# Seven loops written out in Python become loops with a counter in an engine's register

## The reference

```
u    = rmsnorm(x) ; proj = u @ w_in                 # q k v, indexer, z, x/B/C, dt
att  = sparse attention over the top-k keys          # prompt, and samples with a paged cache
y    = Mamba-2 scan of x, B, C, dt, gated and normed
h    = x + concat(att, y) @ w_out
f    = rmsnorm(h)
h    = h + (silu(f @ w_gate) * (f @ w_up)) @ w_down  # hidden width 5632
out  = rmsnorm(h)
```

## Time and profile before

| | |
|---|---|
| median of three runs | 3165.68 us |
| the profiled execution | 3167.28 us, the highest of the three |
| its span, first to last instruction | 3164.5 us |
| outside the span | 2.8 us |
| instructions recorded | 51192 |
| PE busy | 2943.7 us, 93% of the span, 20687 matmuls and as many weight loads |
| DVE busy | 1495.3 us, 47% |
| ACT busy | 950.1 us, 30% |
| POOL busy | 547.6 us, 17% |
| DMA | 352.87 MB, mean 112 GB/s |

### The profile page before, as it was taken

How to read it: one execution, slowest core, us unless ns; L and a number is a source line. 1 busy time by engine, 2 the same in 40 slices (tenths; PEclk the granted TensorE clock), 3 DMA queues, 4 the chain that set the end, 5 groups by cost and what they waited for, 6 DMA issues and landing times.

```text
span 3164.5 us, 51192 instructions
## 1 busy us (share of the span) xinstructions
PE 2943.7 (93%) x20687; PEld 2783.8 (88%) x20687; DVE 1495.3 (47%) x2285; ACT 950.1 (30%) x1442; POOL 547.6 (17%) x230
## 2 busy tenths in 40 slices
PE   6999997799999998699689999999999999999997
PEld 5887897677787877499689999999999999999997
DVE  2322598523434333211576767676676752323223
ACT  4223211222222222222334343343434332222222
POOL 1322232111111110034100000000000023334332
PEclk8999999789999888699899999999999999999999
DMA  6422223443454442443222333333232352232321
GB/s 192 112 65 74 82 88 89 119 133 105 114 149 132 132 126 78 155 135 125 76 88 99 119 101 109 118 100 114 96 122 96 116 197 110 96 122 107 113 96 60
DMA packets 366470, 352.87 MB, mean 112 GB/s; under 512 B 40669, under 2 KB 320261, under 8 KB 365016
## 3 DMA queue, kind: packets, MB, share of 16 engines
q1 hardware_dynamic: 333272, 324.61, 32.5%
q10 hardware_dynamic: 33024, 25.77, 2.5%
HBM read 302.59 MB, written 49.13 MB: 111 GB/s over the span
## 4 chain that ended last, share of the span: by engine, by line
PE 55%; issue 35%; POOL 7%; DVE 2%; ACTq 1%; ACT 1%; POOLq 0%; DVEq 0%
PE PS L1222 31%; PE PS L1204 18%; PE PS L797 6%; POOL WL L700 4%; POOL WL L729 3%; ACTq L1266 0%; DVE XR L2250 0%; ACTq L1267 0%; DVE xo_t L2255 0%; DVE xo_x L2255 0%; DVE y_out L2325 0%; POOL WL L721 0%; ACT WRAW L1275 0%; DVE rstd L2243 0%; PE PS L812 0%
## 5 line engine op out<-in xcount | busy, mean ns | idle before, releaser
L797 PE MATMUL PS<-AH,WH 128*128 128x288 f32 (+1 forms) x2208 | 494.0, 306 | 22.4 <-DVE AL L2152 7.2
L1204 PE MATMUL PS<-H,WH 128*128 128x288 f32 x2816 | 489.4, 296 | 0.7 <-DVE us L2217 0.7
L797 PE MATMUL PS<-AL,WH 128*128 128x288 f32 (+1 forms) x2208 | 482.1, 301 | 0.0
L797 PE MATMUL PS<-AH,WL 128*128 128x288 f32 (+1 forms) x2208 | 481.6, 300 | 0.0
L719 POOL TENSOR_TENSOR WL<-WRAW,WH 128x1024 fp32r<-128x1024 f32 x88 | 214.1, 2433 | 1378.6 <-ACT WH L712 1378.6
L1204 PEld LDWEIGHTS PS<-H,WH 128*128 128x128 f32 x2816 | 414.5, 189 | 0.9 <-issue 0.9
L797 PEld LDWEIGHTS PS<-AH,WH 128*128 128x128 f32 (+1 forms) x2208 | 365.8, 194 | 47.9 <-issue 30.0
L1222 PE MATMUL PS<-xo_t,WH 128*128 128x288 f32 x1888 | 380.2, 296 | 8.6 <-ACT kept L1623 7.6
L797 PEld LDWEIGHTS PS<-AL,WH 128*128 128x128 f32 (+1 forms) x2208 | 365.2, 194 | 0.0
L797 PEld LDWEIGHTS PS<-AH,WL 128*128 128x128 f32 (+1 forms) x2208 | 364.5, 193 | 0.0
L2311 DVE TENSOR_TENSOR XD<-PS,XD 128x576 f32<-128x576 f32 x176 | 133.4, 758 | 398.8 <-PE PS L1204 398.8
(11 more groups left out here) (346 smaller groups left out, 4005.3 us busy)
## 6 DMA issues: line engine op xcount, KB each, us to landing
WRAW<-in_w_gate SPq DMA_DIRECT2D x22, 2048.0 KB
WRAW<-in_w_up SPq DMA_DIRECT2D x22, 2048.0 KB
WRAW<-in_w_down SPq DMA_DIRECT2D x22, 2048.0 KB
WRAW<-in_w_in SPq DMA_DIRECT2D x14, 2048.0 KB, 8.6
raw<-in_w_in SPq DMA_DIRECT2D x48, 512.0 KB, 4.1
kca<-in_cache_k SPq DMA_DIRECT2D x256, 64.0 KB, 2.0
vca<-in_cache_v SPq DMA_DIRECT2D x256, 64.0 KB, 2.0
WRAW<-in_w_out SPq DMA_DIRECT2D x16, 1024.0 KB
```

The lines of the kernel that those rows point to most:

```text
L797: last = nc.tensor.matmul(G[gslot][0:width, h, 0:HALF], wt[:, half, k % 8, 0:width], act[:, (k + shift) % KT, h * HALF:(h + 1) * HALF], st ...
L1204: last = mm(G[(slot + t) % 2][:, h, 0:HALF], wt[:, half, 2 * k + t, :], hid[:, m, k, h * HALF:(h + 1) * HALF], start=(k == 0 and wt is WH ...
```

## The change

Seven `for ... in range(...)` become `with engine.Fori(...) as ...`: one on SP, two each on PE, ACT and DVE. The bodies stay as they are, with the loop variable now a register's value. POOL's loops aren't touched. The order of matmuls, casts, subtractions and DMAs on every engine is the same as before, turn for turn.

```diff
@@ SP, load and store of the gate and up stage @@
-            for p in range(1, NPAIR // 2):
+            with sp.Fori(1, NPAIR // 2) as p:
                 for f, w in enumerate(("w_gate", "w_up")):
                     sp.wait_ge(s["p_lo"], 14 * p + (7 * f - 7))
                     to_slot(f, columns(w, p * 256))
@@ PE, gate and up @@
-            for it in range(NPROD // 42):
+            with pe.Fori(0, NPROD // 42) as it:
                 for n in range(42):
                     seventh(42 * it + (14 + n), 6 * it + (14 + n) // 7, n % 7, (14 + n) % 3, n // 7 % 2)
@@ PE, down @@
-            for it in range((NG - 2) // 2):
+            with pe.Fori(0, (NG - 2) // 2) as it:
                 group_pe(2 * it + 1, 1)
                 group_pe(2 * it + 2, 0)
@@ ACT, gate and up @@
-            for it in range(NPROD // 42):
+            with act.Fori(0, NPROD // 42) as it:
                 for n in range(42):
                     d = LOOP0 + n
@@ ACT, down @@
-            for it in range((NG - 2) // 2):
+            with act.Fori(0, (NG - 2) // 2) as it:
                 group_act(2 * it + 1, 1)
                 group_act(2 * it + 2, 0)
@@ DVE, gate and up @@
-            for it in range(NPROD // 42):
+            with dve.Fori(0, NPROD // 42) as it:
                 for n in range(42):
                     d = LOOP0 + n
@@ DVE, down @@
-            for it in range((NG - 2) // 2):
+            with dve.Fori(0, (NG - 2) // 2) as it:
                 group_dve(2 * it + 1, 1)
                 group_dve(2 * it + 2, 0)
```

## The result

The changed kernel takes 3203.74 us (median of 4 timed executions, 3195.51 to 3205.27), the kernel before 3166.1 us in the same comparison, 37.6 us less. Twelve timed executions of the changed kernel are on record in all, 3193.21 to 3206.7 us, their median 3200.0. The ratio on record is 1.011, with a 95% interval of 1.0095 to 1.0126: 35 us slower, 30 to 40. Forecast was 3175.6 us, 9.9 us slower, with a range of 3164 to 3187. Slower was right; the size was off by a factor of three and a half.

A forecast was written before the change was run, and what follows sets the result against it. PE's matmuls were taken as the bound, with nothing to win. Register operations and other branches cost 0 us; six pauses of 1.65 us at PE's first loop added 9.9 us to 3165.68, giving 3175.6 us, range 3164 to 3187.

The forecast's parts named there:

- The bound: Gate and up and down stretches: PE is busy throughout with unchanged matmuls, so nothing can be won there.
- Register operations on PE, DVE and ACT: In the changed loops: operations of about 0.05 us hide behind queued work and cost 0 us.
- The slack for j = 3: Between DVE's low part and PE's first weight load, even q: 0.27 us becomes 0.17, PE doesn't wait.
- Which loops miss: PE's first loop (8.2 blocks) misses at six branches back; its down loop (6.2 blocks) and other engines' loops stay.
- the rival of nine misses: PE's down loop misses at its three branches too: 14.9 us, 3180.5 us in all; chance 0.20.
- M, the fetch: At PE's first loop's branch back: fetching the missing block takes 3.4 us, PE pauses 1.65 us, six times 9.9 us.
- The upper bound: For the block fetch at PE's first loop's branch: at most 4.1 us, the time of a 512 KB load.
- The clock: In the gate and up stretch: granted clock stays at 1.00, PE at 100% between pauses; no cost counted.
- The signs in the profile: Gate and up: six pauses of 1 to 2.4 us, 42 products apart; none in down; q8's 130 packets well under 110.

The follow-up runs named there:

- e2: Changed kernel with PE's loop over the gate and up products written out, all other register loops kept; ratio 0.9994 to the kernel before.
- e7: As e2, with 215 long-fulfilled waits ahead of PE's products, moving its down loop 0.42 of a block; ratio 1.0023 to the kernel before.
- e8: As e2, with 430 long-fulfilled waits ahead of PE's products, moving its down loop 0.84 of a block; 3205.34 us in one execution.
- e11: Changed kernel with PE's first loop begun eight products later, five branches back on idle DMA engines; ratio 1.003 to the kernel before.
- e3: Changed kernel with PE's first loop begun four products later, five branches back on idle DMA engines; ratio 1.0036 to the kernel before.
- e1: Kernel before with only PE's loop over the gate and up products made a register loop; ratio 1.0104 to the kernel before.
- e4: Changed kernel with 84 products instead of 42 in PE's first loop body, two branches back; ratio 1.0038 to the kernel before.
- e5: Changed kernel with one of eight k steps left out per product of PE's first loop, body 1838 instructions; 3101.43 us, no longer the layer.
- e9: Changed kernel with PE's first loop begun ten products later, five branches back on idle DMA engines; ratio 1.0096 to the kernel before.
- e10: Control: changed kernel with PE's first loop begun seven products later, five branches back under a weight load; ratio 1.01 to the kernel before.
- e6: Changed kernel with two of eight k steps left out per product of PE's first loop, body 1586 instructions; 2992.81 us, no longer the layer.

## Why the prediction was wrong

**The bound** (PE alone, no gain to be had) held: e2 shows it, with the same matmuls in the same stretches.

**Register operations on PE, DVE and ACT: 0 us** held. The slack for j = 3 went from 0.27 us to 0.21 us, forecast 0.17: DVE's low part starts at 1683.84 and takes 1.23 us, PE's load follows at 1685.27.

```profile
1683.84 1.23 DVE L2168 TENSOR_TENSOR WL<-raw_l,WH 128x1024 fp32r<-128x1024 f32 x1 [1.12 <-ACT WH L1615]
```

```profile
1685.27 0.32 PEld L1222 LDWEIGHTS PS<-xo_t,WH 128*128 128x128 f32 x2
```

**Which loops miss** held: PE's first, six times, and not the down loop, nor those of DVE, ACT and SP. It was in part luck: the rows reached to 4.6 blocks, and where between there and 8.2 the limit lies was taken, not read. (The 8.2 goes by 256 instructions a block, which is what the trace of before shows; by the 260 that the text worked out it would be 8.0.) Nor did the text count on the position: in e7, with the down loop 107 instructions further on than in e2, it stays, and in e8, with 215, it misses, as in the rival of nine misses.

**M, the fetch: this step failed.** It was put at 3.4 us, at most 4.1 us. Without a load of weights that was about right: e11's branches take 3.4 to 3.9 us and its pauses 1.4 to 2.0 us, where a pause of 1.65 us was forecast. The text did see that `w_up`'s load was under way at the branch, and allowed 0.2 us for it. The runs show 2 us: 5.3 to 5.7 us, pauses of 3.4 to 3.9 us. The upper bound was at fault too. The landing time of a 512 KB load says how long that load takes, not how long a single 16 KB packet waits behind others: at the first branch 1.0 MB of `w_up` was still to come. Six pauses came to 22.1 us instead of 9.9.

**The clock, a term left out.** "PE at 100% between the pauses, and the clock at 1.00" was wrong. Behind a branch with pauses of 1.4 to 2.5 us in all it never fell (ten branches, e3 and e11). With 3.4 to 5.0 us in all it fell behind 30 of 33 (four of six in the changed kernel, five of six in e1, all in e4, e5, e8, e9 and e10), for 3.4 or 6.8 us, at 1.5 to 2.6 us lost. By e3 and e11 pauses of 1.65 us would have brought no fall, so this term follows from the first. In the profiled execution it is 6.1 of the 28.2 us. How much of the larger loss of the timed executions it is stays open.

**The signs in the profile.** Six pauses, 42 products apart, ahead of a j = 0, and none in the down product: right. That q8's packets would be cut to well under 110 was wrong: there are 125, since the loop fetches all its blocks at every turn.

On the figures of the Trainium skill (Runtime: NRT & Kernel Launch, section Instruction fetch mechanics): 128 KiB in blocks of 16 KiB agrees with e5 to e8 if the block fetched ahead counts as one of the eight. Read as a limit of 2048 instructions for a loop it doesn't, since 1838 missed, and 1588 missed or not by position. The sentence of the Trainium skill that two blocks are held doesn't agree with the down loop's seven, which branched back in 0.22 us without a packet, nor with L1172. The 64 entries that the Trainium skill gives for TensorE's queue (Advanced Engine Details and Errata, section Engine Queue Depths) didn't show: PE ran dry about 2.1 us after each branch began, 16 or 17 pairs.

## What to carry to other kernels

A register loop on an engine that is the bound is free only if its whole body, counted in blocks from where it happens to lie and with one block more, stays where the engine reads its instructions; here that was eight blocks of 256 instructions on PE. Above that, every branch back stalled, and code added far ahead of the loop could decide it (e8). If such a loop must be had, put its branch where the DMA engines are idle and its first instructions well ahead of a block's end: in this kernel that took the cost of a branch from 4.7 us (changed kernel) or 6.2 us (e10) to 1.7 us (e11). Fewer and longer turns help as well (e4), and no loop at all costs nothing. On the engines with slack, and with bodies of at most 204 instructions, the loops cost nothing and gained nothing but a shorter program.

## What the runs showed of the hardware

- PE keeps eight blocks of 16 KB, 256 instructions each, the one fetched ahead among them: a loop that touches seven branches back in 0.21 to 0.23 us without a packet (e6, e7), one that touches eight fetches all of them again at every turn (e5, e8).
- A fetch of 16 KB of instructions waits for the data transfers in flight: the branch took 3.3 to 3.9 us with the DMA engines at a share of 0.02 to 0.04, and 5.3 to 5.7 us where they were at 1.0 to 1.1 in its first 3.2 us. The block's packet began 0.9 to 1.6 us after the branch in the one case, 2.8 to 3.2 us in the other.
- Behind a branch with pauses of PE of 3.4 to 5.0 us in all the granted clock fell to 0.50 in 30 of 33 cases, for 3.4 or 6.8 us, which cost 1.5 to 2.6 us on top of the pause. With 1.4 to 2.5 us in all it fell in none of ten (e3, e11).
- A taken branch to an instruction a few places ahead of a block's end costs two fetches, one after the other (e9: a pause of 1.3 to 1.8 us, one weight load, a pause of 2.8 to 3.1 us).
